# A hybrid decoder layer on one core: decode softmax inside the last gate tile, the second head's parts copied an iteration ahead, smaller groups of key products, narrower gate and convolution columns

## The reference

```python
xn = rms_norm(x, attn_norm_w)
q, k, v, qi, ki, wi, cx, cb, cc, ga, gc = jnp.split(xn @ w_in, split_at, axis=-1)
q = rope(rms_norm(q.reshape(B, T, N_HEADS, HEAD_DIM), q_norm_w), pos)
k = rope(rms_norm(k.reshape(B, T, N_HEADS, HEAD_DIM), k_norm_w), pos)
...
attn = attend(q, k, v, qi, wi, ki)      # top 256 keys by indexer scores, softmax, values
u_hist = jnp.concatenate([conv_prev, cc * cx], axis=1)
conv_out = cb * causal_dwconv(u_hist, conv_w)
mixed = jax.nn.sigmoid(ga) * (attn @ w_o_attn) + jax.nn.sigmoid(gc) * (conv_out @ w_o_conv)
h = x + mixed @ w_merge
g, val = jnp.split(rms_norm(h, ffn_norm_w) @ w_up, [D_FF], axis=-1)
y = h + (jax.nn.silu(causal_dwconv(g_hist, ffn_conv_w) + ffn_conv_b) * val) @ w_down
```

## Time and profile before

| what | before |
|---|---|
| median of 3 runs | 1825.11 us |
| lowest and highest of them | 1823.59, 1825.22 us |
| the profiled execution | 1826.9 us |
| its span, first to last instruction | 1825.1 us |
| TensorE busy | 1749.8 us, 96% |
| VectorE, ScalarE, GpSimd busy | 59%, 32%, 38% |
| mean granted clock of TensorE | 0.975 |

### The profile page before, as it was taken

One profiled execution on the slowest core, in us unless ns is written; L12 is line 12 of the kernel. 1 busy time (PEld: TensorE's weight loads), 2 busy tenths in 40 slices (PEclk: granted clock), 3 DMA queues, 4 the chain that ended last, 5 costly groups with the idle time before them and its releaser, 6 DMA issues.

```text
span 1825.1 us, 29623 instructions
## 1 busy us (share of the span) xinstructions
PE 1749.8 (96%) x10989; PEld 1682.3 (92%) x10989; DVE 1085.2 (59%) x1798; ACT 592.5 (32%) x842; POOL 697.9 (38%) x349
## 2 busy tenths in 40 slices
PE   7999999999998898898999999999999999999998
PEld 5968999999998688887999999999999999999998
DVE  5579999998999455566342344344344344344344
ACT  4755542322112377675212232112112112112110
POOL 3405752553986366563122233223223223223220
PEclk9999999999999799899999999999999999999999
DMA  5221112113775322223233222111111101102102
GB/s 189 85 63 36 46 47 83 59 60 135 243 233 167 116 70 71 70 77 124 94 129 117 69 70 70 47 45 48 46 36 56 46 28 64 45 26 67 40 6 98
DMA packets 58510, 146.90 MB, mean 80 GB/s; under 512 B 14602, under 2 KB 14730, under 8 KB 58298
## 3 DMA queue, kind: packets, MB, share of 16 engines
q1 hardware_dynamic: 52642, 125.21, 21.5%
q10 hardware_dynamic: 5072, 16.37, 2.6%
q0 software_dynamic: 720, 4.33, 0.6%
HBM read 126.09 MB, written 19.89 MB: 80 GB/s over the span
## 4 chain that ended last, share of the span: by engine, by line
PE 57%; issue 14%; POOL 12%; DVE 10%; ACT 5%; DMA 1%; SPq 1%; ACTq 0%; DVEq 0%; POOLq 0%
PE PS L534 17%; PE PX L965 13%; PE PS L917 9%; PE PS L872 5%; POOL WLO L1457 4%; PE PS L788 3%; DVE S L1794 2%; POOL DLO L1616 2%; POOL TG L1612 2%; DVE M L1792 2%; PE PS L758 2%; PE PS L855 2%; DVE LD L1774 2%; PE PX L771 2%; POOL HKL L1545 1%
## 5 line engine op out<-in xcount | busy, mean ns | idle before, releaser
L1457 POOL TENSOR_TENSOR WLO<-WRAW,WHI 128x1024 fp32r<-128x1024 f32 x102 | 256.9, 2519 | 529.1 <-ACT WHI L1007 529.0
L917 PE MATMUL PS<-X2H,WHI 128*128 128x344 f32 (+1 forms) x1032 | 330.4, 320 | 0.3 <-POOL WLO L1457 0.3
L917 PE MATMUL PS<-X2L,WHI 128*128 128x344 f32 (+1 forms) x1032 | 330.4, 320 | 0.0
L917 PE MATMUL PS<-X2H,WLO 128*128 128x344 f32 (+1 forms) x1032 | 330.1, 320 | 0.0
L534 PE MATMUL PS<-XH,WHI 128*128 128x352 f32 x984 | 320.5, 326 | 8.6 <-POOL WLO L1457 7.2
L534 PE MATMUL PS<-XL,WHI 128*128 128x352 f32 x984 | 318.9, 324 | 0.0
L534 PE MATMUL PS<-XH,WLO 128*128 128x352 f32 x984 | 318.8, 324 | 0.0
L1794 DVE MATCH_REPLACE8 S<-M,S 128x1024 f32<-128x1024 f32 (+3 forms) x224 | 206.5, 931 | 0.0
L534 PEld LDWEIGHTS PS<-XH,WHI 128*128 128x128 f32 x984 | 185.9, 189 | 18.4 <-issue 8.8
L1792 DVE MAX8 M<-S 128x8 f32<-128x1024 f32 (+3 forms) x224 | 201.2, 936 | 0.4
L1995 DVE TENSOR_TENSOR HX<-HX,PX 128x344 f32<-128x344 f32 x264 | 135.4, 513 | 108.1 <-PE PX L965 108.1
(11 more groups left out here) (281 smaller groups left out, 3205.3 us busy)
## 6 DMA issues: line engine op xcount, KB each, us to landing
WRAW<-wtiles SPq DMA_DIRECT2D x93, 512.0 KB, 3.6
KR<-cache_k SPq DMA_DIRECT2D x64, 256.0 KB, 3.0
RING<-cache_v SPq DMA_DIRECT2D x64, 256.0 KB, 2.9
DRAW<-wdown SPq DMA_DIRECT2D x11, 1024.0 KB, 4.9
gates<-EV ACTq DMA_DIRECT2D x13, 528.0 KB, 3.9
WRAW<-wtiles ACTq DMA_DIRECT2D x10, 512.0 KB, 5.4
XT<-xT SPq DMA_DIRECT2D x8, 528.0 KB, 8.9
SGA<-gates SPq DMA_DIRECT2D x8, 528.0 KB, 3.6
```

Source lines behind the costliest of these rows:

```text
L917: last = nc.tensor.matmul(PS[b][:, c, 0:n], w[b][:, kk, :], x[:, kk, t0 + c * n:t0 + (c + 1) * n], start=(kk == 0 and p == 0), stop=(kk == ...
L1457: nc.gpsimd.tensor_tensor(WLO[b][:, :, :], WRAW[b][:, :, :], WHI[b][:, :, :].bitcast(F32), ALU.subtract).then_inc(w_lo[b], 1)
```

## The change

Four edits:

- The two early gate tiles, the 12 convolution tiles and the 14 gate tiles take columns 10 to 1047 (`C0:T`, three banks of 346) instead of all 1056. What is computed from them (evacuations, convolution sums, stored gates and convolution outputs, their loads) takes the same 1038 columns. The first columns are of meta tokens whose output isn't returned.
- GpSimd's last groups of key products are 5, 4, 3 instead of 6, 5, 6; the five pages left over are done after the low half of tile 42.
- The decode softmax moves ahead of the attention. The mask of block 8 is made first. TensorE makes the decode logits after two of the three banks of tile 42, VectorE takes their maximum ahead of logits(0, 0), ScalarE sets the queries apart after tile 41's sigmoid, makes the decode exponential, then tile 42's sigmoid, then the copies. `QA`, `PD` and `PTN` lie in key buffers that are free by then.
- For iterations 1 to 3 ScalarE copies head 1's three parts in units 16 and 17 of the iteration before and in unit 0, GpSimd makes the low parts in unit 17, 0 and 1. Iteration 0 stays as it is. GpSimd's first iteration is written out, so that it can differ.

```diff
-        QA = at("QA", [P, 4, 64], 16384)
+        QA = at("QA", [P, 4, 64], 116736)
-        PD = at("PD", [64, TP], 17408)
-        PTN = at("PTN", [LR, 64], 21632)
+        PD = at("PD", [64, TP], 110592)
+        PTN = at("PTN", [LR, 64], 117760)
...
-                            last = nc.tensor.matmul(PS[b][:, c, 0:CH], w[b][:, kk, :], x[:, kk, c * CH:(c + 1) * CH],
+                            last = nc.tensor.matmul(PS[b][:, c, 0:n], w[b][:, kk, :], x[:, kk, t0 + c * n:t0 + (c + 1) * n],
...
             for j in range(12):
-                proj(1 - j % 2, 8 + (j + 1) // 2, XH, XL)
+                proj(1 - j % 2, 8 + (j + 1) // 2, XH, XL, t0=C0, n=CW)
...
-            with pe.Fori(1, 8) as i:
-                proj(1, 13 + i, XH, XL)
-                proj(0, 14 + i, XH, XL)
-
-            pe.wait_ge(ps_free[1], 21)
+            def decode_logits():
+
+                pe.wait_ge(k_red, NS * PAGES)
+                pe.wait_ge(s8_c, 2)
+                pe.wait_ge(ps_free[1], 21)
+                pe.wait_ge(qa_c, 8)
...
+            def decode_turn():
+
+                pe.wait_ge(r_nrm, 9)
+                pe.wait_ge(d_exp, 1)
...
+            with pe.Fori(1, 7) as i:
+                proj(1, 13 + i, XH, XL, t0=C0, n=CW)
+                proj(0, 14 + i, XH, XL, t0=C0, n=CW)
+            proj(1, 20, XH, XL, t0=C0, n=CW)
+            proj(0, 21, XH, XL, t0=C0, n=CW, mid1=decode_logits)
+            decode_turn()
+
             pe.wait_ge(ps_free[0], 22)
...
-                    decode = u == 0 and i == 0
-                    if decode:
-                        decode_logits()
-                    elif more(u + 3):
+                    if more(u + 3):
                         qk(u + 3, i)
                     pv(u, i, extra)
-                    if decode:
-                        pe.wait_ge(d_exp, 1)
-                        qk(u + 3, i)
-                        decode_turn()
...
             qk(0, 0)
             qk(1, 0)
+            pe.wait_ge(d_c, 4)
+            pe.wait_ge(d_z, 2)
             turn(0, 0)
...
-                                nc.scalar.activation(TC[w][:, :], U[:, w:w + TP], ACT.Copy,
+                                nc.scalar.activation(TC[w][:, C0:T], U[:, C0 + w:T + w], ACT.Copy,
...
-                nc.scalar.activation(v3(dst[:, :]), ps_all[b], ACT.Sigmoid).then_inc(ps_free[b], 1)
+                nc.scalar.activation(v3(dst[:, C0:T]), ps_c[b], ACT.Sigmoid).then_inc(ps_free[b], 1)
...
-            gate(1, 20, 7, None)
-            gate(0, 21, 7, None, GLAST, g_last)
-
             def queries_apart():
 
-                nc.scalar.mul(HQ[1][:, TP:NB * P], CK[:, 0:NB * P - TP], 0.0)
+                act.wait_ge(k_red, NS * PAGES)
                 step(nc.scalar.mul(QA[:, :, :].rearrange("p j c -> p (j c)"), CK[:, 0:256], 0.0))
...
+            gate(1, 20, 7, None)
+            queries_apart()
+            decode_expo()
+            gate(0, 21, 7, None, GLAST, g_last)
+            decode_evac()
...
-                    if isinstance(i, int) and i == 0 and u == 0:
-                        decode_expo()
-                        decode_evac()
                     q, later = pages_ahead(u, last)
                     if q is not None:
                         value_high(q, i + later)
-                    if u in HEAD_1:
-                        head_part(i, 1, HEAD_1.index(u))
+                    if isinstance(i, int) and i == 0:
+                        if u in HEAD_1:
+                            head_part(i, 1, HEAD_1.index(u))
+                    elif u == 0:
+                        head_part(i, 1, 2)
+                    if u >= 16 and not last:
+                        head_part(i + 1, 1, u - 16)
...
-            queries_apart()
+            nc.scalar.mul(HQ[1][:, TP:NB * P], CK[:, 0:NB * P - TP], 0.0)
...
-                    if u - 1 in HEAD_1:
-                        head_low(i, 1, HEAD_1.index(u - 1))
+                    if isinstance(i, int) and i == 0:
+                        if u - 1 in HEAD_1:
+                            head_low(i, 1, HEAD_1.index(u - 1))
+                    elif u < 2:
+                        head_low(i, 1, u + 1)
+                    if u == 17 and not last:
+                        head_low(i + 1, 1, 0)
...
-            for n, pages in zip(range(N_GATE + 2, N_O), (2, 6, 6, 5, 6, 5, 6, 6, 5, 6, 5, 6)):
+            for n, pages in zip(range(N_GATE + 2, N_O), (2, 6, 6, 5, 6, 5, 6, 6, 5, 5, 4, 3)):
                 key_products(g, g + pages)
                 g += pages
                 lo(n % 2, n // 2)
+            key_products(g, NS * PAGES)
...
-            for b in range(2, NB):
+            for b in (8, 2, 3, 4, 5, 6, 7):
                 s = S[0:ROWS[b], S_OFF[b]:S_OFF[b] + S_W[b]]
-                nc.vector.tensor_scalar(s, s, 0.5 * TAKEN, NEG, ALU.is_gt, ALU.mult)
+                ins = nc.vector.tensor_scalar(s, s, 0.5 * TAKEN, NEG, ALU.is_gt, ALU.mult)
+                if b == 8:
+                    ins.then_inc(s8_c, 1)
...
+            decode_max()
             logits(0, 0)
+            decode_lows()
             dve.wait_ge(g_dma[0], 112)
             logits(1, 0)
```

More of the change, by code:

```diff
@@ L523, in _, with proj @@
         def _(pe):
-            def proj(b, k, xh, xl, mid=None, extra=None, kn=KD, mid1=None):
+            def proj(b, k, xh, xl, mid=None, extra=None, kn=KD, mid1=None, t0=0, n=CH):
                 pe.wait_ge(w_lo[b], k + 1)
@@ L800, in attend @@
                         turn(u + 1, i)
-                    decode = u == 0 and i == 0
-                    if decode:
-                        decode_logits()
-                    elif more(u + 3):
+                    if more(u + 3):
                         qk(u + 3, i)
                     pv(u, i, extra)
-                    if decode:
-                        pe.wait_ge(d_exp, 1)
-                        qk(u + 3, i)
-                        decode_turn()
[L812 to L834, removed]
-                    for p in range(4 * g, 4 * g + 4):
-                        last = nc.tensor.transpose(PX[g][:, (p % 4) * 64:(p % 4 + 1) * 64], PD[:, p * P:(p + 1) * P],
-                                                   CK[0:64, C_ID:C_ID + 64])
-                    if g == 1:
-                        last = nc.tensor.transpose(PX[1][0:LR, 256:320], PD[:, 8 * P:8 * P + LR], CK[0:64, C_ID:C_ID + 64])
-                    last.then_inc(d_t, 1)
-                pe.wait_ge(d_c, 4)
-                pe.wait_ge(d_z, 2)
             def decode_values(u, i):
@@ L1295, in queries_apart, with decode_expo, decode_evac @@
                                        QKT[e * HD:(e + 1) * HD, 4 + j, TPR:T]).then_inc(qa_c, 1)
+            def decode_expo():
+                act.wait_ge(d_p, 1)
+                nc.scalar.activation(PD[:, 0:PAST + LR], PS[1][0:64, :, :].rearrange("p c t -> p (c t)")[:, 0:PAST + LR], ACT.Exp,
+                                     bias=SM[0:64, 56:57], scale=HD ** -0.5, accum_out=SM[0:64, 57:58]).then_inc(d_exp, 1)
+            def decode_evac():
+                act.wait_ge(d_exp, 1)
+                nc.scalar.copy(SM[64:P, 57:58], SM[0:64, 57:58]).then_inc(d_c, 1)
+                for g in range(2):
+                    act.wait_ge(d_t, g + 1)
+                    nc.scalar.copy(PZ[:, 4 * g:4 * g + 4, 0:64], PX[g][:, 0:256].rearrange("p (a c) -> p a c", a=4)).then_inc(d_c, 1)
+                nc.scalar.copy(PTN[:, :], PX[1][0:LR, 256:320]).then_inc(d_c, 1)
+            gate(1, 20, 7, None)
[3 more added lines that the diff above has]
+            decode_evac()
             def t_evac(u, i):
@@ L1377, in _ @@
                 act.wait_ge(co_in[j], 16)
-                nc.scalar.copy(COH[:, j, :], CRAW[j][:, :]).then_inc(co_h, 1)
+                nc.scalar.copy(COH[:, j, C0:T], CRAW[j][:, C0:T]).then_inc(co_h, 1)
             for t in range(NB):
@@ L1593, in _ @@
                 value_low(q, 0)
-            with pool.Fori(0, 3) as i:
+            attend(0, False)
+            with pool.Fori(1, 3) as i:
                 attend(i, False)
```

67 lines of the change are left out of this document (36 added, 31 removed).

## The result

The changed kernel takes 1807.2 us (median of 4 runs, 1805.4 to 1808.6), the one before 1824.9 (4 runs, 1823.6 to 1825.2): ratio 0.9898, 95% interval 0.9886 to 0.9910, 17.7 us faster. I had said 1793, and 1785 to 1806: the direction holds, the gain is a little over half of what was forecast, and the time lies outside the range. The profiled execution took 1806.2 us, its span is 1804.4.

What follows compares the result with a forecast made beforehand. TensorE, busy 96% of the span, bounds the kernel where it idles or runs at its lower clock. 18.0 + 13.6 + 0.1 = 31.7 us off the 1825.1 median gives 1793 us, range 1785 to 1806.

Steps and rivals of the forecast that it cites:

- Gates' end: Tile 42: decode products 5.8 us at full clock, last third 3.8; TensorE ends at 604.9 us instead of 607.7.
- Rival 1: Gates end later: clock falls after tile 41's wait, or decode products run at 0.50; 1.8 to 7.6 us dearer; chance 0.18.
- Wait before tile 41: TensorE waits 1.6 us there, left of 5.3; no clock fall counted, 1.8 us kept for the range.
- Narrow columns: Convolution and gate tiles at 346 columns a bank: 0.11 us a tile, 2.9 us for TensorE over 26 tiles.
- The chain to unit 3: Attention start: value pages end last, table loads covered; unit 3's exponential at 616.4 us instead of 633.59.
- the 18.0: Gain in us up to the end of the first iteration's key part, taken from 17.2 to 18.6.
- Second head ahead: Iterations 1 to 3, before unit 9: 6.9 us of waits and 6.7 of low clock go, together 13.6.
- I count nothing: Copies moved to the iteration boundaries, where ScalarE is tight: no net cost or gain put into the sum.
- 1 us an iteration at worst: Upper bound on the loss from ScalarE's copies at the iteration boundaries.
- rival 2: Unit 9's wait only moves to the boundary, clock low longer: 13.6 us lost, 1807, or less if partial; chance 0.12.

Runs made afterwards that it cites:

- e2: Changed kernel with one or two decode page products after every three matmuls of tile 42's last bank; ratio 0.9917 to the kernel before.
- e1: Changed kernel with decode logits behind tile 42, turned between qk(0) and qk(1), exponential behind the sigmoid; ratio 0.9875 to the kernel before.
- e6: Changed kernel with decode logits behind tile 42, out(17) behind the next iteration's logits(2), last key groups 5, 5, 2, 5; ratio 0.9810, 1791.6 us.
- e7: Changed kernel with decode products mixed into tile 42's last bank, out(17) later, sigmoid first, first unit's logits ahead of decode transposes; ratio 0.9859, 1799 us.
- b2: Kernel before with only the key product groups 5, 4, 3 and SyncE's wait for the last key sum; ratio 0.9970, 5.5 us faster.
- e3: Changed kernel with head 1's copies of iterations 1 to 3 back in units 1 to 4; ratio 0.9946 to the kernel before.
- b4: Kernel before with narrower columns, key groups, head copies and SyncE's wait, but without the decode softmax's move; ratio 0.9914.
- b3: Kernel before with the head copies alone; ratio 0.9952, 8.8 us faster.
- e4: Changed kernel with VectorE's out(17) behind logits(2) of the next iteration; ratio 0.9846 to the kernel before, 1798.0 us.

## Why the prediction was wrong

**Gates' end (the step that failed most).** I priced the 22 decode products at half of their time at 0.50, 5.8 us, because "amid a busy tile the near row is full clock", and the last third at 3.8. They took 8.8 and 6.3: 5.5 us more, the greater part of A's 8.4. What was wrong above all was to take the clock from the neighbours, as if the products left it alone. The price at 1.00 was too low as well: a pair takes 0.36 us there, more than half of the 0.62 at 0.50. In e2, at 1.00 throughout, products and bank took 10.8 us, of which 24 full matmuls are 3.8, so the products took about 7.0 and not 5.8. By that, 1.2 of the 5.5 us are price and 4.3 are clock. e1 shows the fall behind the tile, e6 without a wait ahead of it, e2 and e7 its absence where full matmuls stand between. Rival 1 had "does the decode products at 0.50", but only for the case that TensorE meets VectorE in mid-tile, and it didn't meet it. Its 5.8 us for that fits the 5.5 by luck: the products were 3.0 dearer, and the bank behind them, which it didn't count, 2.5.

**Wait before tile 41.** 1.6 us and no fall were counted, with 1.8 kept for the range; it was 2.2, and the clock was at 0.78 for 7.8 us, 1.7 more. The two pages came from memory later than worked out (product at 569.32 after 3.51 us of waiting for DMA, ended 571.8), so that tile 41's low half was ready 120.4 us behind the mark and not 119.6. With both, TensorE reached the decode products at 595.07, on the predicted 595.3 only because the execution's mark came early by 2.9. Counted from the mark they began 141.3 us behind it and not 138.6: 2.7 of A's 8.4. Rival 1 named the fall, at 1.8 us. Behind the waits of 2.04 to 2.55 us that eight profiles have at this place the clock was 0.78 to 0.80 for 7.8 us, behind b2's 1.80 it was 1.00. The length of a wait doesn't settle it: the same 1.84 us at the second boundary were followed by 0.67 in the kernel before and by 1.00 in b2 and e3. That the loss could be avoided is shown by e6.

**Narrow columns.** Predicted 2.9 us; alone 0.9 (-0.7 to 2.6). The narrower gate tiles lengthened the wait behind them (6.4 us) where the kernel still had it. What is left of the 2.9, some 1.8 us, is too small for these measurements.

**The chain to unit 3.** Right, relative to the gates: value pages ended last, 8.2 us behind the gates' end (610.2 to 618.45; 7.8 predicted), unit 3's exponential 3.4 us after the first value copy (3.7 predicted). The two table loads were covered. Their rows show 1.28 us each, the second beginning with the end of the copy before it and the exponential following at once. The Trainium skill ("ScalarE: Activation LUTs", What ACT_TABLE_LOAD costs) puts a drain beside the load, 2.66 us in all; this trace shows none.

**What the decode move was worth.** 2.9 us (b4), because it lengthened the TensorE path by almost what it took out of the attention: the last sigmoid of the gates is 11.3 us later from the mark than in b4 (156.5 after 145.2), and the way from there to unit 3's exponential is 14.3 us shorter (11.6 after 25.9). I had not separated it from the other parts of the 18.0.

**Second head ahead.** The waits went as predicted, one of 1.9 us is left in the first iteration, and e3's 9.4 us shows them return. B is 9.6 us shorter in b3, and with the 5.1 it lost at the boundaries that is 14.7, near the 13.6 of the prediction. The periods of the changed kernel's iterations are 53.4 and 53.7 us (731.28 less 677.90, 784.93 less 731.28) and not 52. The failed step is "I count nothing" for the boundary: it cost 5.1 us against the kernel before (b3), as much as B's whole 5.0, and 8.5 against e3, where the boundaries run at 1.00. The bound "1 us an iteration at worst" took only ScalarE's time into account; the cost was TensorE's clock. That is the milder rival 2, which gave no figure of its own, and its condition held: TensorE idled there already. (That the measured time is the 1807 of its full form is luck: the waits didn't move, and more than half of the loss lies in A.) The copies did their damage only with VectorE's order at the boundary (out(17) first): e4 keeps the copies and changes the order, e3 keeps the order and takes the copies back, and both stay at 1.00 at all three boundaries. At the first boundary the copies show as a wait of 1.06 us for ScalarE's exponential, where it was 0.5. Why at the second the clock stays low for longer behind the same 1.84 us of idling, and why it falls there in the kernel before and not in b2 or e3, stays open: no run moved the copies to other units.

**The rest.** 0.5 us of the span's difference lies behind B and is not explained. The mark's 2.9 us the other way is variation between executions.

## What to carry to other kernels

Moving small products into the middle of a dense stretch doesn't give them that stretch's clock: look at what a whole run of them does, and price the dense work that follows at the low clock as well. When work is moved to a place where the engine with the tightest time already waits, look first at which engine's order makes it wait there; here a change of VectorE's order was worth more (9.5 us) than the whole decode move (2.9). And an edit that makes tiles shorter ahead of a wait for another engine gives its gain to the wait.

## What I had not expected of the hardware

The granted clock fell to 0.50 with TensorE busy throughout, behind eight to eleven pairs of small products, both inside the tile (at 598.70) and behind it (at 605.75 in e1, at 601.5 in e6). It stayed at 1.00 for 10.7 and 10.8 us where full matmuls stood between the same products. The Trainium skill ("TensorE: Matmul & The Clock Gate", HAM oscillation — how this bites in real kernels) speaks of gaps in which the engine stands still; these rows show a fall without a gap. In the other direction, 1.06 us of idling at a boundary (e4) and 1.8 before tile 41 (b2) left the clock at 1.00, and 1.84 us at the second boundary left it there in two kernels (b2, e3) and not in the one before.
